# Attention scores contracted over 64 partitions in two row groups of TensorE, with a second copy of q and k whose halves are exchanged

## The reference

```python
s = jnp.einsum("bqhmd,bkhmd->bhmqk", qi, k).astype(jnp.float32) * scale   # scale = 64 ** -0.5
p = jax.nn.softmax(s, axis=-1)
a = p[:, :, 0] - lam * p[:, :, 1]
return jnp.einsum("bhqk,bkhe->bqhe", a.astype(v.dtype), v)
...
o = rms_norm(o, subln_g) * (1.0 - lam_init)
```

## Time and profile before

| | |
|---|---|
| median of 3 runs | 4265.45 us (4264.38 to 4270.08) |
| the profiled execution, its own time | 4266.51 us |
| its span, first to last instruction | 4264.5 us |
| mean granted TensorE clock | 0.959 of 2.4 GHz |
| attention, from its first score matmul to the output projection | 2606.5 to about 3155 us of the span |

### The profile page before, as it was taken

The page is one execution under the profiler, slowest core; times in us unless marked ns, Lnnn a source line. Parts: engine busy times, 40 slices in busy tenths (PEclk is TensorE's granted clock), DMA queues, the critical chain, the costliest instruction groups (busy, mean ns, idle before and its releaser), DMA issues.

```text
span 4264.5 us, 53100 instructions
## 1 busy us (share of the span) xinstructions
PE 3938.3 (92%) x21940; PEld 2935.4 (69%) x21940; DVE 1844.0 (43%) x4800; ACT 782.5 (18%) x1790; POOL 309.1 (7%) x455
## 2 busy tenths in 40 slices
PE   6979999799987999999979999898999699999996
PEld 2435455644446999999965545666654699999996
DVE  5432012665234444444423314777743444444442
ACT  1112000111020111111120003555532111111112
POOL 0000000000010010011010000010101011111101
PEclk8989999999998999999989999999999799999998
DMA  8750101232334777777760111000013387777776
GB/s 309 250 203 21 40 37 73 79 123 97 120 116 152 270 267 266 262 262 270 254 215 20 40 45 35 1 1 1 1 55 120 127 269 262 262 262 261 264 250 220
DMA packets 281314, 659.18 MB, mean 155 GB/s; under 512 B 9432, under 2 KB 9809, under 8 KB 277810
## 3 DMA queue, kind: packets, MB, share of 16 engines
q1 hardware_dynamic: 245202, 517.05, 33.7%
q0 software_dynamic: 35872, 138.74, 10.6%
HBM read 595.05 MB, written 60.70 MB: 154 GB/s over the span
## 4 chain that ended last, share of the span: by engine, by line
PE 84%; DVE 7%; ACT 5%; DMA 2%; issue 2%; POOL 0%; SPq 0%; DVEq 0%; ACTq 0%; POOLq 0%
PE ps L1005 24%; PE ps L754 13%; PE ps L1024 12%; PE ps L926 6%; PE ps L757 6%; PE ps L723 3%; PE ps L861 3%; PE ps L877 3%; ACT hT L1334 2%; PE ps L1068 2%; PE ps L1069 2%; PE ps L972 1%; PE ps L964 1%; ACT hT L1179 1%; DVE gst L1846 1%
## 5 line engine op out<-in xcount | busy, mean ns | idle before, releaser
L1005 PE MATMUL ps<-big,ring 128*128 128x144 f32 x8192 | 1020.4, 287 | 3.5 <-DVE big L1780 3.5
L1005 PEld LDWEIGHTS ps<-big,ring 128*128 128x128 f32 x8192 | 1010.3, 191 | 9.0 <-issue 8.5
L754 PE MATMUL ps<-hT,ring 128*128 128x384 f32 x1728 | 559.6, 487 | 5.5 <-issue 5.5
L1024 PE MATMUL ps<-big,ring 128*128 128x144 f32 x4096 | 518.0, 288 | 0.0
L1024 PEld LDWEIGHTS ps<-big,ring 128*128 128x128 f32 x4096 | 508.5, 191 | 0.8
L754 PEld LDWEIGHTS ps<-hT,ring 128*128 128x128 f32 x1728 | 328.9, 190 | 235.7 <-issue 8.3
L1780 DVE TENSOR_SCALAR big<-ps,amul,modc 128x128 f32<-128x128 f32 (+1 forms) x512 | 136.4, 342 | 378.9 <-PE ps L973 378.9
L1288 ACT ACTIVATE big<-ps 128x144 f32<-128x144 f32 x256 | 74.5, 291 | 1129.6 <-PE ps L1005 1129.6
L1802 DVE TENSOR_TENSOR big<-big,ps 128x144 f32<-128x144 f32 x256 | 77.9, 304 | 425.1 <-ACT big L1288 421.4
L1846 DVE TENSOR_REDUCE gst<-ps 128x1 f32<-128x1152 f32 x144 | 177.6, 1233 | 168.5 <-PE ps L1070 168.2
L926 PE MATMUL ps<-ring,yT 128*128 128x512 f32 x576 | 247.5, 592 | 0.0
(11 more groups left out here) (312 smaller groups left out, 4142.6 us busy)
## 6 DMA issues: line engine op xcount, KB each, us to landing
ring<-in_moe_wg SPq DMA_DIRECT2D x64, 2048.0 KB, 10.7
ring<-in_moe_wu SPq DMA_DIRECT2D x64, 2048.0 KB, 13.3
ring<-in_moe_wd SPq DMA_DIRECT2D x64, 2048.0 KB, 11.1
ring<-in_w_mod SPq DMA_DIRECT2D x24, 2048.0 KB, 11.2
big<-aff_t POOLq DMA_DIRECT2D x32, 576.0 KB, 4.1
ring<-in_w_in_even SPq DMA_DIRECT2D x7, 2048.0 KB, 7.7
big<-x_res POOLq DMA_DIRECT2D x27, 512.0 KB, 8.4
ring<-in_w_in_odd SPq DMA_DIRECT2D x6, 2048.0 KB, 8.9
```

The costliest lines, as they stand in the source:

```text
L754: i = mm(ps[:, b + g, 0:384], w[:, k, c * P:(c + 1) * P], hTv[:, k, g * 384:(g + 1) * 384], start=k == 0, stop=k == DK - 1)
L1005: last_mm = mm(ps[:, 3 + f % 2, g * CAP:(g + 1) * CAP], w[u - n0][:, k, c * P:(c + 1) * P], xsT[ee][:, k, :], start=k == 0, stop=k == DK - 1)
L1024: last_mm = mm(ps[:, 3 + d % 2, 0:CAP], w[4 + d // 4][:, k, (d % 4) * P:(d % 4 + 1) * P], hid[:, k, :], start=k == 0, stop=k == DK - 1)
```

## The change

The score matmuls are done in two row groups of TensorE: a matmul with `tile_position=(0, 0)` uses the upper 64 partitions, one with `(64, 0)` the lower 64. For map m, keys 0 to 511 are multiplied in the map's own row group, from `qTa` and `kTa` as they lie; keys 512 to 1023 in the other row group, from copies `qTs` and `kTs` in which the 64-partition halves are exchanged; the 128 cached keys again in the own group. The copies are made by four transfers per head, issued by GpSimd, into a ring slot that is kept for the whole attention (`swap_unit`), double-buffered over heads. The zero-padded `qz` and its 144 GpSimd copies are gone.

Further: q is scaled by 0.125 when it leaves PSUM, so the exponential needs no scale; the maximum is negated inside the reduction; the first map's 1/sum0 no longer scales the 1152 exponentials but the 128-wide output, and sum0 is multiplied into the second map's factor instead.

```diff
+        swap_unit = unit(None)
...
+        swap = slot(swap_unit)[:, 0:3072].rearrange("p (b n) -> p b n", b=2)
+        kTs = [swap[:, b, 0:512] for b in range(2)]
+        qTs = [swap[:, b, 512:1536] for b in range(2)]
...
+            def swap_halves(h):
+                b = h % 2
+                if h >= 2:
+                    pool.wait_ge(*at("a.s", 2 * (T * (h - 2) + 8)))
+                for lo in (0, 64):
+                    to, of = slice(lo, lo + 64), slice(64 - lo, 128 - lo)
+                    ld(qTs[b][to, :], qTa[of, h, 0:LAT], f"a.sw{b}")
+                    ld(kTs[b][to, :], kTa[of, h, 512:LAT], f"a.sw{b}")
...
-                    pe.wait_ge(*at("a.qz", n + 1))
-                    lhs = qz[:, n % 2, m, :]
                     if q < 8:
-                        mm(ps[:, 3 * m, :], lhs, kTa[:, h, 0:512], start=True, stop=True)
-                        mm(ps[:, 3 * m + 1, :], lhs, kTa[:, h, 512:1024], start=True, stop=True)
-                        i = mm(ps[:, 3 * m + 2, 0:P], lhs, ckT[:, h, :], start=True, stop=True)
+                        pe.wait_ge(*at(f"a.sw{h % 2}", 64 * (h // 2 + 1)))
+                        near, far = slice(64 * m, 64 * m + 64), slice(64 - 64 * m, 128 - 64 * m)
+                        own, other = qTa[near, h, q * P:(q + 1) * P], qTs[h % 2][far, q * P:(q + 1) * P]
+                        mm(ps[:, 3 * m, :], own, kTa[near, h, 0:512],
+                           start=True, stop=True, tile_position=(64 * m, 0))
+                        mm(ps[:, 3 * m + 1, :], other, kTs[h % 2][far, :],
+                           start=True, stop=True, tile_position=(64 - 64 * m, 0))
+                        i = mm(ps[:, 3 * m + 2, 0:P], own, ckT[near, h, :],
+                               start=True, stop=True, tile_position=(64 * m, 0))
...
-                        i = A(dst, ps[:, b:b + 3, 0:384], ACT.Copy)
+                        i = A(dst, ps[:, b:b + 3, 0:384], ACT.Copy, scale=0.125 if j < 8 else 1.0)
...
-                        ch(nc.vector.tensor_reduce(gstf[:, c + m:c + m + 1], bank(3 * m, 3)[:, 0:w], AX.X, ALU.max))
-                        ts(gstf[:, c + 2 + m:c + 3 + m], gstf[:, c + m:c + m + 1], -0.125, None, ALU.mult
-                           ).then_inc(s("a.nm"), 1)
+                        nc.vector.tensor_reduce(gstf[:, c + 2 + m:c + 3 + m], bank(3 * m, 3)[:, 0:w], AX.X, ALU.max,
+                                                negate=True).then_inc(s("a.nm"), 1)
...
-                    ch(tt(gstf[:, c + 7:c + 8], gstf[:, c + 7:c + 8], lamc[:, 4:5], ALU.mult))
+                    ch(stt(gstf[:, c + 7:c + 8], gstf[:, c + 4:c + 5], gstf[:, c + 7:c + 8], lamc[:, 4:5],
+                           ALU.mult, ALU.mult))
-                    ch(ts(e0, e0, gstf[:, c + 6:c + 7], None, ALU.mult))
...
-                    cp(o[:, q, :], ps[:, 7, 0:P]).then_inc(s("a.oev"), 1)
+                    ts(o[:, q, :], ps[:, 7, 0:P], gstf[:, r:r + 1], None, ALU.mult).then_inc(s("a.oev"), 1)
```

More of the change, by code:

```diff
@@ L301, in build @@
         ohs = [oh, misc[:, 0:1152].rearrange("p (t d) -> p t d", t=T)]
-        qz = misc[:, 1152:1664].rearrange("p (b m t) -> p b m t", b=2, m=2)
+        swap = slot(swap_unit)[:, 0:3072].rearrange("p (b n) -> p b n", b=2)
+        kTs = [swap[:, b, 0:512] for b in range(2)]
+        qTs = [swap[:, b, 512:1536] for b in range(2)]
         junk2 = misc[:, 1664:1792]
@@ L406, in load @@
                     sp.wait_ge(*at(f"slot{n % NS}_free", n // NS))
+                if n == swap_unit:
+                    sp.sem_inc(s(f"slot{n % NS}_landed"), 16)
+                    return
                 dst = slot(n) if len(src.shape) == 2 else slot(n).rearrange("p (k n) -> p k n", k=src.shape[1])
@@ L596, in _ @@
             ld(misc[:, 0:2048].rearrange("p (a n) -> p a n", a=2), tab["rope"], "a.rope")
[L598 to L605, removed]
+            def swap_halves(h):
[6 more added lines that the diff above has]
+                    ld(kTs[b][to, :], kTa[of, h, 512:LAT], f"a.sw{b}")
             pool.wait_ge(*at("q.rope", 16))
+            landed(pool, swap_unit)
+            swap_halves(0)
             ld(ckrow, a["cache_k"][0, 0].rearrange("t h d -> t (h d)"), "a.ck")
[L609 to L612, removed]
+            swap_halves(1)
             pool.wait_ge(*at("q.mm", 34))
@@ L620, in _ @@
             pool.wait_ge(*at("a.kctx_out", 16))
-            for n in range(2, len(steps)):
-                queries(n)
+            for h in range(2, AH):
+                swap_halves(h)
             after_mixer(1)
@@ L1062, in scores @@
                     h, q = steps[n]
-                    pe.wait_ge(*at("a.qz", n + 1))
                     if n:
                         pe.wait_ge(*at("a.e", 2 * (n - 1) + m + 1))
-                    lhs = qz[:, n % 2, m, :]
                     if q < 8:
-                        mm(ps[:, 3 * m, :], lhs, kTa[:, h, 0:512], start=True, stop=True)
-                        mm(ps[:, 3 * m + 1, :], lhs, kTa[:, h, 512:1024], start=True, stop=True)
-                        i = mm(ps[:, 3 * m + 2, 0:P], lhs, ckT[:, h, :], start=True, stop=True)
-                    else:
-                        i = mm(ps[:, 3 * m, 0:P], lhs, kTa[:, h, LAT:NT], start=True, stop=True)
+                        pe.wait_ge(*at(f"a.sw{h % 2}", 64 * (h // 2 + 1)))
[7 more added lines that the diff above has]
+                               start=True, stop=True, tile_position=(64 * m, 0))
+                    else:
+                        near = slice(64 * m, 64 * m + 64)
+                        i = mm(ps[:, 3 * m, 0:P], qTa[near, h, LAT:NT], kTa[near, h, LAT:NT],
+                               start=True, stop=True, tile_position=(64 * m, 0))
                     i.then_inc(s("a.s"), 1)
@@ L1122, in attention @@
                 pe.wait_ge(*at("a.tev", head_tev[-1]))
+                pe.sem_inc(s(f"slot{swap_unit % NS}_free"), 1)
             pe.wait_ge(*at("f.spec", 18))
@@ L1333, in exps @@
                         c = (n % 4) * 8
-                        A(eb[:, n % 2, m, 0:w], bank(3 * m, 3)[:, 0:w], ACT.Exp, scale=0.125,
+                        A(eb[:, n % 2, m, 0:w], bank(3 * m, 3)[:, 0:w], ACT.Exp,
                           bias=gstf[:, c + 2 + m:c + 3 + m], accum_out=gstf[:, c + 4 + m:c + 5 + m]
@@ L1881, in attention @@
                     o = ohs[h % 2]
-                    cp(o[:, q, :], ps[:, 7, 0:P]).then_inc(s("a.oev"), 1)
+                    r = (n % 4) * 8 + 6
+                    ts(o[:, q, :], ps[:, 7, 0:P], gstf[:, r:r + 1], None, ALU.mult).then_inc(s("a.oev"), 1)
                     dve.wait_ge(*at("a.oev", n + 1))
```

## The result

| | before | after |
|---|---|---|
| median | 4266.32 us (4264.38 to 4270.08, 4 runs) | 4191.58 us (4184.26 to 4192.67, 4 runs) |
| span of the profiled execution | 4264.5 us | 4190.2 us |
| attention: first score matmul to output projection | 548.3 us | 471.2 us |

The ratio is 0.982, 95% interval 0.9803 to 0.9837: 74.7 us less, where 61 were forecast (4205, range 4178 to 4238). In the traces attention ran from 2606.55 to 3154.84 us before and runs from 2607.28 to 3078.46 now, 77 us less. The rest of the span ran some 3 us longer, so all of the gain lies in attention.

A forecast was written before the change was run, and what follows sets the result against it. Plain turns were taken as bound by TensorE (6.90 us) and a DVE and ACT loop (7.03), becoming 5.98. 64 steps x 0.92 = 59, less 1.6 for context steps, gave 4208, with boundary gains 4205; range 4178 to 4238.

The forecast's parts named there:

- Two bounds: A plain attention turn has two bounds, TensorE 6.90 us and a DVE and ACT loop 7.03; the change shortens both.
- Side by side: Score matmuls in two row groups run concurrently: a map's scores take 1.08 us against 1.94, saving 0.86.
- Borders: Tiling changes around scores on TensorE: entering 0.20 us, leaving 0.19 to 0.20; two of each per turn, 0.80.
- The loop of DVE and ACT: Dropping the 1152-wide scaling and two one-element products takes 1.22 us from the 7.03 loop, leaving 5.81 per turn.
- Boundary and context steps: Latent steps at head boundaries gain 0.92 us like plain ones; each of 8 context steps loses 0.2, together 1.6.
- Transfers: Four transfers per head for the exchanged halves, perhaps 10 us, are hidden before use; without cover they would cost 70.
- Clock: No clock drop in plain turns; one more drop per head at the boundaries would cost 14 us.
- 1 (strict order): Rival, chance 0.12: score passes start strictly in program order, turn 6.40 us, gain 0.50, time 4235.
- 2 (no side by side): Rival, chance 0.10: row groups do not run concurrently, turn 7.70 us, time 4298.
- 3 (cheaper borders): Rival, chance 0.16: borders cost less than taken, the DVE and ACT loop holds the turn at 5.81 us, time 4186 to 4196.
- 4: Rival, chance 0.08: the clock drops more often at head boundaries, adding 8 to 25 us, time 4213 to 4230.
- 5: Rival, chance 0.02: the exchanged halves arrive late, giving up to 70 us back, time about 4270.

The follow-up runs named there:

- groups-only run: Row groups and exchanged halves of the change, with DVE's and ACT's arithmetic of the kernel before: 4237.58 us, ratio 0.9937 to the kernel before.
- one-group run: Changed kernel, but keys 512 to 1023 also multiplied in the map's own row group, after keys 0 to 511: 4340.81 us, ratio 1.0183.
- the run with the partner last: Changed kernel with the other row group's matmul issued last, behind the own group's four passes: 4184.56 us, ratio 0.9814.

## Why the prediction was right

**Two bounds.** Right, and the main point: 6.90 on TensorE and 7.03 on DVE and ACT. Each half alone brought 25 and 20 us, and the chain in the groups-only run is the 7.02 loop. But before the change the 7.03 loop held turns only at the start of attention; from head 1 on DVE and ACT held TensorE up at the boundaries and behind the context steps, not in plain turns.

**Side by side.** Right: 0.86 per map, taken from column groups of line 675, held for row groups. The one-group run gives it back exactly, 7.56 per turn.

**Borders.** Right in kind, one term too large. Entering cost 0.09 and 0.1 for the weights, as taken (0.20). Leaving was taken as 0.19 to 0.20, from line 699, where 0.10 was for the weights. Here the first matmul behind the scores is a turned block: it starts 0.09 after the stream's end, and its first block costs some 0.05 more (the next score stretch starts 1.02 later, at 2644.26, for eight blocks of 0.11 and an entry of 0.09). So leaving costs 0.14, two exits 0.28 instead of 0.40, and the turn is 5.84 instead of 5.98. The forecast took all 64 latent steps for plain turns; the traces have 26, and in these the missing 0.14 is 3.6 us.

**The loop of DVE and ACT.** Forecast 5.81, measured 5.85 where it shows by itself. The 3-operand product, costed like its predecessor, takes 0.22 instead of 0.16.

**Boundary and context steps.** Costed like plain steps or at a small loss, and here lies most of what the forecast missed. Between the first and the last product with v the time fell by 73.7 us:

| turns | forecast at 0.92, context -0.2 | measured |
|---|---|---|
| 26 plain ones | 23.9 | 28.7 |
| 24 around the context steps | 13.1 | 18.9 |
| 21 at the heads' boundaries | 19.3, or up to 5 more | 26.1 |

The three turns around a context step were 4.46, 7.60 and 6.03 us and are 4.52, 5.95 and 4.91: the two latent ones gained 1.65 and 1.12, not 0.92. The start and the end of attention gave another 3.4, and the rest of the span took 2.8 back. The single terms were thus all a little low, and the allowance for the boundaries (4208 less 5 would be 4203; the forecast says 4205) was too small.

**Transfers.** Right: hidden. A transfer landed in 3.8 us (median), the four of a head were issued within 2.2 us, about a head before their use, and TensorE never waited for them.

**Clock.** Right: plain turns at 1.00, and 0.95 over attention against 0.96 before. In the one-group run the mean was 0.86 with the same borders; its plain turns stayed at 1.00 too, and the loss stood at the boundaries.

**Rivals.** 1 (strict order) was refuted, as to the starts, by the run with the partner last. 2 (no side by side) would have been the slower side: its mechanism, forced, gave 4340.81, above the 4298 that I had worked out, by the clock and by steps that I had counted as relieved. 3 (cheaper borders) is the one whose time came true: 4191.58 lies in its 4186 to 4196 and outside the forecast's own 4197 to 4213, though inside the stated range. Its mechanism is half true: leaving was cheaper by a third, but the turn is held by TensorE at 5.84, between the forecast's 5.98 and the rival's 5.81, and the rest of the 75 us came from the steps that are not plain. That the time fits the rival so well is partly luck. 4 and 5 did not occur.

## What to carry to other kernels

Before costing a faster engine, look for the loop that does not touch it: here TensorE's 6.90 and a 7.03 loop of DVE and ACT lay almost level, either half of the change brought about a third of the whole, and both together brought all of it. Before multiplying a plain turn's gain by the number of steps, count how many steps are plain: here 26 turns of 71. Half-height contractions pay only as pairs in different row groups, and each switch between row groups and the full array costs 0.14 to 0.19 us here, so keep such matmuls in one stretch and pair them with like lengths. Where no row shows an operation, the nearest relative in the same trace (column groups here) can price it, with the border costs read from the same place. An edit that moves a wait can make a bound of its own, as the output copy's did, so compare the engine's own work with the turn that it gets.

## What the runs showed that I had not expected

- A matmul in another row group starts ahead of three passes issued before it (0.01 us after the first, in the run with the partner last), so the order within a stretch does not change the starts. Its signal, though, comes only after those of the passes before it.
- In a single row group the granted clock was at half for some 170 us of attention, against 47 with pairs; 39 us of the 149 between the two kernels.
- Two stretches of scores joined into one took 2.13 us from their start (2635.94) to the next turned block (2638.07) instead of 2 x 1.28: map 1's own group is map 0's other group, so the unequal lengths even out.
